# Projections of r, k and v in the scan as 64x64 quarters in two PSUM banks, added by VectorE; scratch ring of two banks instead of three

## Chip, cores and metric
One core of one Trainium2 chip. The metric is device time in microseconds (us); the kernel before takes 3047.45 us (median of 3 runs, 3044.28 to 3048.7).

## What is computed
A two-block network on 512 tokens of width 1024 (plus 256 context tokens), all in float32. Only the first block's scan is touched:

```python
# centred_shift: z[t-1]*w[0] + z[t]*w[1] + z[t+1]*w[2], over z = h @ w_in
r, k_f, k_b, v, d_f, d_b, kk, a_f, a_b, dg = rwkv_prep(centred_shift(z_rwkv, p["shift_conv"]), p)
# per token, 16 heads of 64, forward and backward:
S_new = S * d_t - (S @ kk_t) (kk_t * a_t)^T + v_t k_t^T
y     = S @ r_t           # forward: of S_new; backward: of S
```

The projection `h @ w_in` for r, k and v is a contraction over 1024 channels. The context needs k and v only. After the scan each head's y is centred, normalised, gets the bonus `sum(r*k*r_k) * v`, and is gated.

## The kernel before
`stage_scan` goes over 8 pairs of heads (`KT = 8`; a pair fills the 128 partitions, one head in each half). `TURNS` are 9 passes. Turn j solves pair j and meanwhile prepares pair b = j+1 and finishes pair a = j-1. A turn has 15 levels (s, l), s in 0..2 and l in 0..4. In each level TensorE, whose program is strictly in order, issues: a product (`multiply`, L759, into INV), the right side of a recurrence step beside scores (L861, L728), then `beside(j, (s, l, 0))`, then `solve` (L901, waits for ScalarE's `negate`, L1195), `correct` (L839, L841, waits for VectorE's `mask`, L1516), `read_out` (L928), then `beside(j, (s, l, 1))`; the next product waits for VectorE's `update` (L1527, L1529). At l = 4 there is no recurrence step; `correct_last` (L821) stands beside `x0` (L824). VectorE's own order is mask, its `beside(.,.,0)`, update, `state`, its `beside(.,.,1)`.

The projections are `project(b, which, piece)`, spread over TensorE's `beside` slots: K_X (k of the 512 tokens) at (0,0,1), (0,1,0), (0,1,1), (0,2,1), two channel groups each; K_V (k and v of the 256 context tokens) at (0,4,1), (1,0,1), (1,1,0), (1,1,1), four each; R_X (r), one group each at (1,4,0), (1,4,1), (2,0,1), (2,1,0), (2,1,1), (2,2,0) after two at (1,3,0); V_X (v) 3, 2 and 3 at (2,3,1), (2,4,0), (2,4,1). Each is a 128x128 matmul accumulating in bank PROJ (L680, L676). `bonus` (L951) follows the K_X piece at (0,1,0), `center` (L957) stands before the K_V piece at (0,4,1). VectorE's `shift` (L405, L408, L411; for K_V L1572, L1575, L1578) reads PROJ three times per projection: K_X at (0,3,0), K_V at (1,2,1), R_X at (2,2,1), V_X at (2,4,1). The next projection waits until all of it is done.

Everything else of TensorE goes through `Scratch` (L479), a ring of three banks: `take` waits until the use that had the bank before was read out ("moved"). A turn's uses in order: tokV0, score, par, score, bonus, score, rate 0 and 1, score, decay 0 and 1, tokB0, rate 2, decay 3, tokK0, x0, rate 3, decay 2, center, tokV1, score, var, tokB1, score, rstd, tokK1, score, gate, tokV2, score, ks, tokB2, x0, tokK2, inverse 0 and 1, scores(b) twice, x0. ScalarE reads tok (L1237), rate (L1213), decay (L1230), x0 (L1259) and center (L1316), VectorE the rest (score: L1600).

The rate and decay products (L643) are 64x64 matmuls with 512 or 256 columns, `w[H[d], half]` by `low[H[d], tokens]`; `H` are the two halves of the partitions, `O` the same two swapped.

Of the kernel before, what the change touches and what calls it, by code (L numbers as in the profile page):

```python
# [7 lines left out]
ALU = mybir.AluOpType  # L8
# [3 lines left out]
P = 128  # L12
T, TC, D = 512, 256, 1024
TA = T + TC
KT = D // P
# [494 lines left out]
def stage_scan(k, hT, w_low, low_loaded, th, da, sg, ya, spare, m, first_chunk, first_loaded, loose):  # L510
# [8 lines left out]
    bank = k.bank  # L519
# [4 lines left out]
    S = {n: k.sem("scan_" + n) for n in names}  # L524
    own_d, own_p = k.sem("scan_dve"), k.sem("scan_pool")
    H = [slice(HEAD * h, HEAD * h + HEAD) for h in range(2)]
    O = H[::-1]
# [3 lines left out]
    with ExitStack() as s:  # L531
        wj = first_chunk[:].rearrange("p j n -> p (j n)")[:, 0:3 * KT * P].rearrange("p (j i c) -> p j i c", j=KT, i=3)
# [18 lines left out]
        rkr = loose[:, 0:2 * T].rearrange("p (a t) -> p a t", a=2)  # L551
        hr = k.sb("head_r_k", [P, P], s)
# [7 lines left out]
        Z = k.sb("Z", [P, 2, 2, HEAD], s)  # L560
        yj, ysq = (loose[:, c:c + T] for c in (2 * T, 3 * T))
        rstd = k.sb("rstd", [P, 2 * NX], s)
        flat = spare[:].rearrange("p n c -> p (n c)")
        by_steps = lambda view: view.rearrange("p (n t) -> p n t", t=HEAD)
        per_step = lambda view: view.rearrange("p (n d c) -> p n d c", d=2, c=HEAD)
# [3 lines left out]
        U = flat[:, 5 * TA:5 * TA + P].rearrange("p (d c) -> p d c", d=2)  # L569
        rn = flat[:, 5 * TA + P:5 * TA + 2 * P].rearrange("p (d c) -> p d c", d=2)  # L570
        ZG = k.sb("ZG", [P, 2, HEAD], s)[:]
        Y, RU, INV, INVT, PROJ = (bank[i] for i in range(5))
        DZ = RU[:, 2 * P:3 * P]
        RIGHT = INVT[:, 2 * P:3 * P]
        sc = Scratch(k, "scratch", bank[5:8])
        block = s.enter_context(nc.Block())

        w_rkv = A["w_in"][0, :, 0:3 * D].rearrange("(i p) (s n c) -> p i s n c", p=P, s=3, n=KT)
# [17 lines left out]
        K_X, K_V, R_X, V_X = range(4)  # L596
        proj_no = lambda j, i: 4 * j + i + 1
        proj_bank = lambda j, i: Y if j == 0 and i in (K_V, V_X) else PROJ
        LOW_DECAY, LOW_RATE, LOW_GATE = range(3)
        low_bank = {LOW_DECAY: (INVT[:], INV[:, TC:2 * TC]), LOW_RATE: (RU[:], INV[:, 0:TC]), LOW_GATE: (RU[:], None)}  # L600
        low_no = lambda f: (6, 12, 15)[f]
        SHIFTED = 15
        shift_no = lambda j, i: SHIFTED * j + (3, 9, 12, 15)[i]

        def steps_of(j, s):

# [16 lines left out]
        def _(pe):  # L623
            mm = pe.matmul
# [32 lines left out]
            def project(j, which, piece, pieces=4):  # L657

                if not live(j):
                    return  # L660
                if piece == 0:
                    if which == K_X:
                        pe.wait_ge(S["wk_loaded"], 16 * (j + 1))
                    elif which == R_X:
                        pe.wait_ge(S["wr_loaded"], 16 * (j + 1))
                    elif which == K_V:
                        pe.wait_ge(S["wv_loaded"], 16 * (j + 1))
                    if j == 0 and which >= R_X:
                        pe.wait_ge(S["shift"], shift_no(0, which - 2))
                    elif j:  # L670
                        pe.wait_ge(S["shift"], shift_no(j, which - 1) if which else shift_no(j - 1, V_X))
                to = proj_bank(j, which)
                if which == K_V:
                    i, o = (1, to[:, 0:TC]) if piece < 2 else (2, to[:, TC:2 * TC])
                    for c in range(4 * (piece % 2), 4 * (piece % 2) + 4):
                        last = mm(o, wj[:, c, i, :], hT[:, c, T:TA], start=(c == 0), stop=(c == KT - 1))  # L676
                else:
                    i = {K_X: 1, R_X: 0, V_X: 2}[which]
                    for c in range(KT // pieces * piece, KT // pieces * (piece + 1)):
                        last = mm(to[:], wj[:, c, i, :], hT[:, c, 0:T], start=(c == 0), stop=(c == KT - 1))  # L680
                if piece == pieces - 1:
                    last.then_inc(S["proj"], 1)
# [264 lines left out]
            def bonus(j):  # L947
                if live(j):
                    pe.wait_ge(S["rk_done"], j + 1)
                    o = sc.take(pe, "bonus", j)  # L950
                    sc.fill(mm(o[:], hr[:], rkr[:, j % 2, :], start=True, stop=True), "bonus", j)  # L951

            def center(j):
                if live(j):
                    pe.wait_ge(S["y_copied"], j + 1)
                    o = sc.take(pe, "center", j)
                    sc.fill(mm(o[:], m["center"][:], yj[:], start=True, stop=True), "center", j)  # L957

            def variance(j):
                if not live(j):  # L960
# [26 lines left out]
            def beside(j, at):  # L987
# [4 lines left out]
                if at == (0, 0, 1):  # L992
                    project(b, K_X, 0)
# [514 lines left out]
        def _(dve):  # L1508
            tt, stt, ts = dve.tensor_tensor, dve.scalar_tensor_tensor, dve.tensor_scalar
# [45 lines left out]
            def shift(j, which):  # L1555

                if not live(j):
                    return
                dve.wait_ge(S["proj"], proj_no(j, which))
                mine = Steps(dve, S["shift"], shift_no(j, which - 1) if which else SHIFTED * j)  # L1560
                taps_of = lambda i: [col(j, 3 * t + i) for t in range(3)]
                z_of = proj_bank(j, which)
                if which == K_X:
                    if j:
                        dve.wait_ge(S["ke_done"], 2 * j)
                    shifted(mine, dve, [(kj[:, XS], z_of[:], T)], taps_of(1))
                elif which == K_V:
                    if j:
                        sc.settled(dve, "tokV", j - 1, 0)
                    parts_ = ((kj[:, CS], z_of[:, 0:TC], taps_of(1)), (vj[:, CS], z_of[:, TC:2 * TC], taps_of(2)))  # L1570
                    for dst, z, w in parts_:
                        mine.then(ts(dst, z, w[1], None, ALU.mult))  # L1572
                    mine.settle()
                    for dst, z, w in parts_:
                        mine.then(stt(dst[:, 1:TC], z[:, 0:TC - 1], w[0], dst[:, 1:TC], ALU.mult, ALU.add))  # L1575
                    mine.settle()
                    for dst, z, w in parts_:
                        mine.then(stt(dst[:, 0:TC - 1], z[:, 1:TC], w[2], dst[:, 0:TC - 1], ALU.mult, ALU.add))  # L1578
                    mine.settle()
                elif which == R_X:  # L1580
                    shifted(mine, dve, [(rj[:], z_of[:], T)], taps_of(0))
                else:
                    if j:
                        sc.settled(dve, "tokV", j - 1, 1)
                        sc.settled(dve, "tokV", j - 1, 2)
                    shifted(mine, dve, [(vj[:, XS], z_of[:], T)], taps_of(2))
# [102 lines left out]
            def gated(j):  # L1689
                if live(j):  # L1690
                    z = sc.read(dve, "gate", j)
                    dve.wait_ge(S["yn_done"], j + 1)
                    sc.free(stt(ya[:, j, :], yj[:], col(j, 13), z[:], ALU.add, ALU.mult), "gate", j)

            def beside(j, at):
                a, b = j - 1, j + 1
# [12 lines left out]
                if at == (1, 1, 1):  # L1709
                    normed(a)  # L1710
                if at == (1, 2, 1):
                    shift(b, K_V)
                if at == (1, 3, 0):
                    gated(a)
                if at == (1, 3, 1):
                    clamp(b)
                if at == (1, 4, 0):
# [1901 lines left out]
```

## Time and profile before

| | |
|---|---|
| median of 3 runs | 3047.45 us |
| profiled execution: its time / its span | 3037.74 us / 3036.0 us |
| TensorE, VectorE, ScalarE, GpSimd busy | 90%, 39%, 20%, 8% of the span |
| turns 0 to 6 of the scan | 135 to 833 us, about 100 us each |
| TensorE, VectorE busy in those | 92.59 and 60.30 us of each turn on average |

A row of the timeline says: start, length, engine, line, operation, out<-in, shape (rows x columns of the weights, then 64x512: partitions x moving columns), count merged in one row, and in brackets how long the engine was idle before it and what ended that. A float32 matmul stands as two MATMUL records (x2 is one matmul), each with its own weight load (PEld). A record's length includes the way through the array, so two that follow closely overlap.

### The profile page before, as it was taken

What the parts mean: (1) busy time and instruction counts of PE and PEld (TensorE: products, weight loads), DVE (VectorE), ACT (ScalarE), POOL (GpSimd) and SP (SyncE); (2) the same over time, 40 slices, a digit from 0 to 9 for tenths busy, and PEclk for the clock granted to TensorE, in tenths of its full rate; (3) what the DMA queues carried; (4) which work ended last, traced back from release to release, by engine and by line L of the source; (5) the groups of instructions that cost most, each with busy time, mean ns of one, the idle gap of its engine ahead of it and who ended that gap; (6) DMA issues with size and microseconds to landing.
All of it is one profiled execution on the core that took longest, in us unless ns stands there. A gap on an engine that the chain in (4) does not pass through costs nothing. (4 is left out here: it accounts for less than half of the span.)

```text
span 3036.0 us, 69543 instructions
## 1 busy us (share of the span) xinstructions
PE 2743.5 (90%) x31106; PEld 1489.7 (49%) x31106; DVE 1180.1 (39%) x2612; ACT 612.1 (20%) x1257; POOL 253.2 (8%) x283
## 2 busy tenths in 40 slices
PE   5899999999979999988988988988986998999998
PEld 3466666776664444444433433433333454455553
DVE  3565566566644762163221221211004245423333
ACT  3233323323321100010000000000002344322222
POOL 1220122112200000001000000000000111110000
PEclk9899999999999999998999999999997999999999
DMA  5000000000006871266999999999994311042210
GB/s 201 24 19 20 19 25 20 21 19 25 20 17 226 301 269 63 72 266 292 430 431 431 431 430 430 429 431 431 430 431 157 126 51 36 0 124 61 62 41 28
DMA packets 191501, 557.42 MB, mean 184 GB/s; under 512 B 32140, under 2 KB 119714, under 8 KB 166646
## 3 DMA queue, kind: packets, MB, share of 16 engines
q1 hardware_dynamic: 191222, 553.19, 46.6%
q8 instruction: 237, 3.88, 0.5%
q14 instruction: 42, 0.34, 0.0%
HBM read 550.65 MB, written 2.24 MB: 182 GB/s over the span
## 5 line engine op out<-in xcount | busy, mean ns | idle before, releaser
L2273 PE MATMUL bank<-arena,xe 128*64 128x512 f32 x1024 | 348.6, 607 | 37.4 <-DMA gates<-in_exp_w_dram 22.6
L680 PE MATMUL bank<-arena 128*128 128x512 f32 x384 | 199.6, 641 | 6.7 <-DVE vj L1578 5.3
L2273 PEld LDWEIGHTS bank<-arena,xe 128*64 128x64 f32 x1024 | 109.3, 140 | 186.8 <-issue 178.2
L3297 PE MATMUL bank<-arena 128*128 128x512 f32 x384 | 176.2, 607 | 3.4 <-PEq L78 3.4
L2273 PE MATMUL bank<-arena,hidT 128*64 128x512 f32 x512 | 170.0, 595 | 0.7 <-DMA gates<-in_exp_w_dram 0.5
L2726 PE MATMUL bank<-arena 128*128 128x512 f32 x320 | 146.4, 607 | 8.1 <-ACT arena L2887 8.1
L2273 PE MATMUL bank<-mg_ring,xe 128*64 128x512 f32 x256 | 116.2, 608 | 19.5 <-DMA u<-in_exp_w_dram 19.5
L2498 DVE TENSOR_TENSOR x<-x,bank 128x512 f32<-128x512 f32 x64 | 43.6, 686 | 230.1 <-PE bank L2311 230.1
L2273 PE MATMUL bank<-ys,xe 128*64 128x512 f32 x256 | 115.9, 607 | 17.8 <-DMA arena<-in_exp_w_dram 17.1
L2491 DVE TENSOR_TENSOR hid<-hid,bank 128x512 f32<-128x512 f32 x32 | 19.8, 682 | 284.4 <-PE bank L2273 284.4
L1516 DVE TENSOR_TENSOR pm<-bank,m_level 128x512 f32<-128x512 f32 x120 | 82.8, 690 | 118.1 <-PE bank L759 117.2
L839 PE MATMUL bank<-pm,XT 64*64 64x32 f32 x3072 | 107.9, 220 | 12.1 <-DVE pm L1516 9.5
L2273 PE MATMUL bank<-gates,xe 128*64 128x512 f32 x256 | 118.1, 616 | 0.0
L2273 PE MATMUL bank<-u,xe 128*64 128x512 f32 x256 | 116.6, 610 | 0.0
L841 PE MATMUL bank<-XT,pm 64*64 64x32 f32 x3072 | 111.5, 222 | 3.1 <-issue 3.1
L3297 PEld LDWEIGHTS bank<-arena 128*128 128x128 f32 x384 | 70.9, 192 | 84.2 <-issue 84.2
L759 PEld LDWEIGHTS bank<-X,px 64*64 64x64 f32 x2560 | 85.8, 135 | 48.9 <-issue 21.4
L759 PE MATMUL bank<-X,px 64*64 64x64 f32 x2560 | 98.3, 224 | 11.5 <-DVE XT L1529 6.5
L839 PEld LDWEIGHTS bank<-pm,XT 64*64 64x64 f32 x3072 | 100.3, 137 | 16.8 <-DVE pm L1516 11.6
L2726 PEld LDWEIGHTS bank<-arena 128*128 128x128 f32 x320 | 60.4, 195 | 82.4 <-issue 73.6
L841 PEld LDWEIGHTS bank<-XT,pm 64*64 64x64 f32 x3072 | 100.1, 136 | 1.5 <-issue 1.5
L680 PEld LDWEIGHTS bank<-arena 128*128 128x128 f32 x384 | 67.5, 196 | 63.1 <-issue 57.2
(523 smaller groups left out, 5513.8 us busy)
## 6 DMA issues: line engine op xcount, KB each, us to landing
arena<-in_exp_w_dram SPq DMA_DIRECT2D x96, 2048.0 KB, 26.7
gates<-in_exp_w_dram SPq DMA_DIRECT2D x24, 2048.0 KB, 29.5
ys<-in_exp_w_dram SPq DMA_DIRECT2D x24, 2048.0 KB, 26.0
mg_ring<-in_exp_w_dram SPq DMA_DIRECT2D x24, 2048.0 KB, 26.2
u<-in_exp_w_dram SPq DMA_DIRECT2D x24, 2048.0 KB, 30.7
ws_w<-in_ada_w_dram SPq DMA_DIRECT2D x40, 1024.0 KB, 5.3
arena<-in_odd_w_in_dram SPq DMA_DIRECT2D x32, 512.0 KB, 4.0
arena<-in_w_in_dram SPq DMA_DIRECT2D x24, 512.0 KB, 4.4
```

The costliest lines, as they stand in the source:

```text
L680: last = mm(to[:], wj[:, c, i, :], hT[:, c, 0:T], start=(c == 0), stop=(c == KT - 1))
L759: last = mm(INV[c, cs(q)], part(4 * g + q // 2, q % 2, 0, 0)[h], X[h, (j * GROUPS + g) % 2, q, :], start=True, stop=True)
L839: mm(into(INV, h, q), XT[c, g, q, :], blocks(pm[c, q, :], b, 0), start=True, stop=True)
L841: last = mm(into(INVT, c, q), pm[c, q, :], blocks(XT[c, g, q, :], b, 1), start=True, stop=True)
L1516: tt(pm[:], INV[:].rearrange("p (q t) -> p q t", q=8), m["level"][:, l, :].unsqueeze(1).to_broadcast([P, 8, HEAD]), ALU.mult).then_inc(S[" ...
L2273: r[e] = mm(out[a, :], lhs[j][:, a], w[:, j, 512 * c:512 * c + 512], start=(first and j == 0), stop=(last and j == len(lhs) - 1), skip_gro ...
L2491: dve.tensor_tensor(hid[:, f, :], hid[:, f, :], bank[4 + f][:], ALU.mult).then_inc(S["hid_made"], 1)
L2498: dve.tensor_tensor(x1[:, n, c], x1[:, n, c], bank[scatter_bank(q, o)][:], ALU.add).then_inc(S["added"], 1)
L2726: last = mm(o[:], w[:, c, i, :], hT[:, i, :], start=(i == 0), stop=(i == KT - 1))
L3297: last = mm(o[:], w[:, i, t, :], hT[:, t, :], start=(t == 0), stop=(t == KT - 1))
```

## The change
From the second pair on, each 128x128 projection matmul becomes four 64x64 ones: the two that stay in their half go to PROJ, the two that cross go to a second bank, PROJ2. `shift` first copies PROJ2 to SBUF (`zsum`), adds PROJ to it, and then does its three steps from `zsum`. The next projection waits only until the copy and the addition are done (`banks_read_no`). PROJ2 is bank 5, so `Scratch` has banks 6 and 7. `bonus` and `center` become two 64x64 matmuls each (their matrices are block diagonal). `gated` goes from VectorE's (1,3,0) to (1,2,1), ahead of the K_V shift. The first pair's projections in the prologue stay as they are.

```diff
+        zsum = k.sb("z_sum", [P, T], s)
-        Y, RU, INV, INVT, PROJ = (bank[i] for i in range(5))
+        Y, RU, INV, INVT, PROJ, PROJ2 = (bank[i] for i in range(6))
-        sc = Scratch(k, "scratch", bank[5:8])
+        sc = Scratch(k, "scratch", bank[6:8])
-        SHIFTED = 15
-        shift_no = lambda j, i: SHIFTED * j + (3, 9, 12, 15)[i]
+        FIRST_SHIFTS, SHIFTS = (3, 9, 12, 15), (5, 13, 18, 23)
+        shift_no = lambda j, i: FIRST_SHIFTS[i] if j == 0 else FIRST_SHIFTS[-1] + SHIFTS[-1] * (j - 1) + SHIFTS[i]
+        before_shift = lambda j, i: shift_no(j, i - 1) if i else shift_no(j - 1, V_X) if j else 0
+        banks_read_no = lambda j, i: before_shift(j, i) + 2 if j else shift_no(j, i)
...
-                        pe.wait_ge(S["shift"], shift_no(j, which - 1) if which else shift_no(j - 1, V_X))
+                        pe.wait_ge(S["shift"], banks_read_no(j, which - 1) if which else banks_read_no(j - 1, V_X))
+                if j:
+                    if which == K_V:
+                        i, out, tokens = (1, slice(0, TC), slice(T, TA)) if piece < 2 else (2, slice(TC, 2 * TC), slice(T, TA))
+                        channels = range(4 * (piece % 2), 4 * (piece % 2) + 4)
+                    else:
+                        i, out, tokens = {K_X: 1, R_X: 0, V_X: 2}[which], slice(0, T), slice(0, T)
+                        channels = range(KT // pieces * piece, KT // pieces * (piece + 1))
+                    for c in channels:
+                        for to, halves in ((PROJ, H), (PROJ2, O)):
+                            for rows, half in zip(H, halves):
+                                last = mm(to[half, out], wj[rows, c, i, half], hT[rows, c, tokens],
+                                          start=(c == 0), stop=(c == KT - 1), skip_group_check=True)
+                    if piece == pieces - 1:
+                        last.then_inc(S["proj"], 1)
+                    return
...
-                    sc.fill(mm(o[:], hr[:], rkr[:, j % 2, :], start=True, stop=True), "bonus", j)
+                    for h in H:
+                        last = mm(o[h, :], hr[h, h], rkr[h, j % 2, :], start=True, stop=True)
+                    sc.fill(last, "bonus", j)
...
-                    sc.fill(mm(o[:], m["center"][:], yj[:], start=True, stop=True), "center", j)
+                    for h in H:
+                        last = mm(o[h, :], m["center"][h, h], yj[h, :], start=True, stop=True)
+                    sc.fill(last, "center", j)
...
-                mine = Steps(dve, S["shift"], shift_no(j, which - 1) if which else SHIFTED * j)
+                mine = Steps(dve, S["shift"], before_shift(j, which))
-                z_of = proj_bank(j, which)
+                z_of = zsum if j else proj_bank(j, which)
+                if j:
+                    mine.last(dve.tensor_copy(zsum[:], PROJ2[:]))
+                    mine.last(tt(zsum[:], PROJ[:], zsum[:], ALU.add))
...
                 if at == (1, 2, 1):
+                    gated(a)
                     shift(b, K_V)
-                if at == (1, 3, 0):
-                    gated(a)
```

## Rows read from the trace of the kernel before

**Rows 1.** Windows, turn 3: length, then busy us (instructions) of each engine, TensorE clock.
```profile
437.70:537.80 100.10, 92.73 (x2789) 68.00 (x2783) 61.21 (x125) 33.79 (x68) 18.77 (x15) 0.98 0.08 22
```

**Rows 2.** Timeline, a slot with one 128x128 matmul of 512 columns between 64x64 ones.
```profile
407.12 0.40 PE L861 MATMUL bank<-Z,qr 64*64 64x64 f32 x8
407.45 1.12 PE L680 MATMUL bank<-arena 128*128 128x512 f32 x2
...
408.51 0.28 PE L901 MATMUL bank<-x,XT 64*64 64x64 f32 x2
```

**Rows 3.** Timeline, a slot with four 64x64 matmuls of 512 columns (rates), same neighbours.
```profile
350.65 0.28 PE L728 MATMUL bank<-qr,kt 64*64 64x128 f32 x2
350.76 1.02 PE L643 MATMUL bank<-da,a2j 64*64 64x512 f32 x6
351.47 0.34 PE L901 MATMUL bank<-x,XT 64*64 64x64 f32 x6
```

**Rows 4.** Timeline, a product (crossing halves) beside values (same halves), 64 columns each.
```profile
406.77 0.23 PE L759 MATMUL bank<-X,px 64*64 64x64 f32 x2
406.79 0.23 PE L944 MATMUL bank<-px,x 64*64 64x64 f32 x2
...
406.83 0.23 PE L759 MATMUL bank<-X,px 64*64 64x64 f32 x2
```

**Rows 5.** Timeline, level (0,1): end of the update and start of the next product.
```profile
446.96 0.42 DVE L1529 TENSOR_TENSOR XT<-XT,bank 128x256 f32<-128x256 f32 x1
...
448.60 0.27 PE L759 MATMUL bank<-X,pc 64*64 64x64 f32 x2
```

**Rows 6.** Groups by line and form, VectorE: count, then busy us, mean ns of one, idle before.
```profile
L186 DVE TENSOR_SCALAR arena<-ws_w,silu_c 128x512 f32<-128x512 f32 x20 | 9.7, 483 | 60.3 <-DMA ws_w<-in_ada_w_dram 60.3
L188 DVE SCALAR_TENSOR_TENSOR arena<-ws_w,silu_c,arena 128x512 f32<-128x512 f32 x120 | 90.2, 752 | 15.6 <-DMA ws_w<-in_ada_w_dram 11.0
L3470 DVE COPY na_k<-bank 128x512 f32<-128x512 f32 x8 | 5.5, 692 | 28.0 <-PE bank L3297 28.0
```

**Rows 7.** Timeline, level (0,3): first of the K_X shift's three steps, and the next product.
```profile
457.19 0.74 DVE L405 TENSOR_SCALAR kj<-bank,pcol 128x512 f32<-128x512 f32 x1
...
460.34 0.27 PE L759 MATMUL bank<-X,pc 64*64 64x64 f32 x2 [0.83 <-DVE XT L1529]
```

**Rows 8.** Timeline, K_V shift at (1,2,1) and what starts after it in (1,3).
```profile
487.13 0.48 DVE L1572 TENSOR_SCALAR kj<-bank,pcol 128x256 f32<-128x256 f32 x1
...
489.85 0.93 ACT L1264 ACTIVATE x<-kj,pcol 128x768 f32<-128x768 f32 x1 [4.77 <-DVE vj L1578]
...
489.97 1.95 PE L680 MATMUL bank<-arena 128*128 128x512 f32 x4 [0.83 <-DVE vj L1578]
...
491.85 0.39 PE L901 MATMUL bank<-x,XT 64*64 64x64 f32 x6
```

**Rows 9.** Waits of TensorE, 135 to 830 us: total us, times, longest us.
```profile
PE bank L839 <- DVE pm L1516: 9.3, 10, 1.7
```

**Rows 10.** Timeline, level (0,2): VectorE reads a score bank; first solve after the rate products.
```profile
450.68 0.69 DVE L1600 TENSOR_TENSOR px<-bank,m_part 128x512 f32<-128x512 f32 x1 [0.20 <-PE bank L728]
...
451.17 0.34 PE L901 MATMUL bank<-x,XT 64*64 64x64 f32 x6
```

**Rows 11.** Timeline, level (0,4): tokK0 on TensorE, reads on ScalarE, center.
```profile
461.70 1.10 PE L744 MATMUL bank<-m_id,kt 64*64 64x64 f32 x32
...
461.95 0.47 ACT L1213 ACTIVATE ra<-bank,pcol 128x256 f32<-128x256 f32 x1 [1.15 <-PE bank L643]
...
463.33 0.59 ACT L1311 ACTIVATE arena<-bank 128x512 f32<-128x512 f32 x1
...
464.56 1.10 PE L957 MATMUL bank<-arena,m_center 128*128 128x512 f32 x2 [0.32 <-ACT X L1259]
```

**Rows 12.** Timeline, level (2,0): the inverse's transposes, and ScalarE's copy of tokK2.
```profile
503.66 0.87 PE L702 MATMUL bank<-ident,x 128*128 128x128 f32 x6
503.95 0.59 ACT L1237 ACTIVATE tokK<-bank 128x512 f32<-128x512 f32 x1
```

## The prediction, made before the result was known
> **What bounds the kernel now.** The page first: the time is the span of one core. The windows of the scan next: a turn takes about 100 us, TensorE shows a record in 93 of them and VectorE in 61 [rows 1]. That looks like a kernel bound by TensorE, but a float32 record is long because of its way through the array, so a wait of up to 0.2 us between two records stays invisible, and the busy share does not say whose lateness decides. That is read level by level from the timeline: what started last before `correct` and before the next product. Two kinds of level appear. In most, TensorE comes late itself: at (0,1) VectorE's update ends at 447.38, the product starts at 448.60, after the K_X piece [rows 5]. There a shorter slot pays in full up to 1.2 us. In the levels that hold a `shift`, VectorE is late: at (0,3) the product waits for the update, which stood behind the shift [rows 7], and `correct` waits for the mask up to 1.7 us, 9.3 us over 10 times [rows 9]; these are the levels after the R_X and V_X shifts, whose three steps run ahead of the next mask. So the scan is a loop between TensorE and VectorE (with ScalarE's evictions in it), and an edit has to be priced in its level.
>
> **What the change takes away.** The 128x128 matmul between 64x64 ones. The last small record before it starts at 407.30 (407.12 + 0.40 less a record of 0.22), the next small one at 408.51: 1.21 us for one matmul [rows 2]. The four quarters of the rates do the same number of multiplications for 512 columns: the small record before them starts at 350.65, the next at 351.47, 0.82 us; the other pair of tiles is free 0.15 us later, so 0.82 to 0.97 us [rows 3]. A slot saves 0.24 to 0.39 us; I take 0.35, nearer to the first, because what follows is free to start on the pair that is free. The saving is per slot, not per matmul: it is the emptying of the array at both edges of the slot, and inside a slot both forms stream alike.
>
> A turn has 18 such slots with projections (K_X 4, K_V 4, R_X 7, V_X 3; `bonus` and `center` share two of them). Not gained: (1,1,0), where the transposes of `rstd` stay 128x128 and keep both edges; (1,3,0), which stands behind the K_V shift (priced below); (1,4,0), after which `x0` waits for GpSimd's work on XT anyway; (2,1,1) and (2,2,0), after which `correct` waits for VectorE's mask. That leaves 13 slots, 4.55 us. `bonus` uses only the tiles that stay in their half and the solve behind it only the crossing ones, so it overlaps: 0.3 us more. Gain 4.85 us a turn.
>
> **What it adds on VectorE.** Before each of four shifts a copy out of PSUM, 0.69 us, and an addition with one operand in PSUM (a mask of that kind takes as long), 0.69 us, with two settling waits of 0.035. Of the three steps the first gets cheaper with its source in SBUF, 0.48 instead of 0.74; the other two stay at 0.75 [rows 6, 7]. That is 1.45 - 0.26 = 1.19 us; upper bound 1.45 if the first step gains nothing. VectorE is busy for only 60% and could hide this, but not where it stands:
> - K_X at (0,3,0): between mask and update, the product already waits for it [rows 7]: 1.19 in full.
> - R_X at (2,2,1): ahead of mask (2,3), the longest wait of `correct` [rows 9]: 1.19.
> - V_X at (2,4,1): ahead of mask (0,0), `correct` just waits for it already: 1.19. (The shift itself starts earlier by what the three V_X slots save; that is in the gain.)
> - K_V at (1,2,1): before, 2.7 us from 487.13 to 489.85 [rows 8]. Now `gated` comes first (0.75), then copy and addition (1.42), then six steps of 256 columns at half the prices of rows 6, about 2.15: end at 491.45 instead of 489.82. Behind it are ScalarE's square of k (0.93) and, in ScalarE's order behind that, `negate` (0.28); the solve starts at 492.75 instead of 491.85 [rows 8]: 0.9. The earlier release of the banks (after the addition, at 489.3) lets R_X start 0.65 us earlier and buys nothing, since the solve waits for `negate`.
>
> Together 4.47 us a turn.
>
> **What two scratch banks add.** With three, a `take` waits for the use three before; with two, for the use two before. TensorE stops at that wait with all its program behind it. Going through the turn's list of uses:
> - (0,2): the rates take both banks at once, the second held by the score written just before. VectorE reads it from 450.68 to 451.37. The rates then start at 451.43 and need 0.9: the solve comes at 452.3 instead of 451.17 [rows 10]: 1.15 us, nothing hides it.
> - (0,4): tokK0 waits for the read of rate 2, to 462.42 (start 462.47 instead of 461.70); `x0` with `correct_last` follows 0.88 later, to 464.3. ScalarE then copies tokK0, Y and x0, 0.59 each, done at 465.4; only then rate 3 and decay 2 may be written, and `center` waits for the read of rate 3 (0.47) until 466.5. Before it started at 464.56 [rows 11]: 1.95 us.
> - (2,0): inverse 1 waits for ScalarE's copy of tokK2, to 504.54, and the array must empty behind it; solve at about 504.95 instead of 504.5 [rows 12]: 0.45.
> - (1,0): `var` waits for the copy of tokV1, the same kind with more between: an estimate of 0.3.
> - par at (0,0) waits for tokV0 and decay 1 at (0,3) for the score, 0.7 and 1.0 us, but in these two levels VectorE's shift is later still: 0. All other takes find the bank free by over 1 us. The move of `gated` is needed for the score at (1,3) and costs what stands above.
>
> Together 3.85 us a turn.
>
> **The sum.** 4.47 + 3.85 - 4.85 = 3.47 us a turn, 7 turns prepare a pair: 24 us. The projections bring four times the instructions (80 MATMUL records become 320, in a turn of 2789 [rows 1]); about 1 us more of stalls in issuing, and 1 us for the ring in the prologue: +26 us. Against the profiled execution 3037.74 + 26 = 3064; the median of the runs lies 9.7 above that execution, so 3073.5.
>
> **One rule set against the trace.** Both pairs of quarters write their two row halves into one bank. In the scan the product does this too (both halves into INV), beside `values` (both into Y): two records of each, four together, every 0.06 us [rows 4], and 64 columns are an eighth of the 0.43 us pass of 512, 0.054. So at 64 columns nothing is serialised. The rates do not test it at 512: each of their banks gets one row half.
> The Trainium skill, "TensorEngine Tiling (Array Packing)", Restrictions and Gotchas, says that different row tiles cannot access the same PSUM bank simultaneously; by this the pair would run one after the other. The trace disagrees at 64 columns; no row shows it at 512. It is the last of the rivals.
>
> **Rivals.**
> - *The ring does not bind.* If the takes find their banks read (readers earlier than the list says, or the stalls fall where TensorE would wait anyway), what is left is 4.47 against 4.85, and against up to 17 x 0.39 + 0.5 = 7.1 if every slot pays: -0.4 to -2.6 us a turn, 3 to 18 us faster, 3037 in the middle. It decides from the point where the ring costs under 0.4 us a turn. For it: most takes are far from binding. Against: (0,2), where the order of the program alone forces 1.15 us.
> - *Balance*: half the ring's cost and slots at 0.39 in nearly all places give 4.47 + 1.9 - 6.3 = 0: 3047.
> - *The edges stay*, the change does not do what it says: quarters of 512 columns mixed with small ones do not close up. Gain near 0: 8.3 x 7 = 58, 3106. Against: rows 3.
> - *Serialised pairs*: each of the 32 column blocks of 512 a turn (16 of 256 count half) takes 0.86 us more: 27.5 x 7 = 193, 3240.
>
> **Chances and range.** Slower as summed 0.70; ring not binding 0.17; balance 0.08; edges stay 0.03; serialised 0.02. Forecast 3073. Its own range by the bounds: gain 13 x 0.24 to 17 x 0.39, VectorE 4.3 to 5.9, ring 3.0 to 4.6: most of it within +9 to +45, 3056 to 3092. The range for 8 in 10 takes in the balance: 3045 to 3092. A difference under 0.2% (6 us) cannot be told from none. Slower by over 0.2% 0.75, within 0.2% 0.08, faster 0.17.
>
> **What would show it.** After: in each turn with projections, copy and addition of 0.69 before every shift; the product at (0,3) and `correct` at (2,3) and (0,0) later behind the shift by 1.2; small matmuls following a quarter slot without the 1.21; the rates at (0,2) starting only when the score is read, `center` about 2 us later after tokK0. The turn should take 103 to 104 us, TensorE's busy share lower. Wrong if the turn is shorter than 100 us, if the rates at (0,2) start within 0.2 us of the scores' end, or if a slot of quarters takes more than 1 us a channel.

## The result and the profile after

The changed kernel takes 3091.4 us (median of 4 runs, 3087.5 to 3096.71), the kernel before, run beside it, 3045.86 us (median of 4 runs). The ratio is 1.0166, 95% interval 1.0147 to 1.0185: 50 us slower, or 45.5 by the medians. The profiled execution took 3089.26 us with a span of 3087.5. Forecast were 26 us more: the direction was right, the size little more than half.

Below, us against the kernel before are the ratio less 1, times 3040. The expectations use differences of medians (58 for e2, 26 for e4), which lie up to 3 us off. A 95% interval reaches 4 to 9 us to either side.

Windows of the kernel after: the same columns as in [rows 1], turn 3 and then the seven turns that prepare a pair.

```profile
449.56:558.23 108.67, 92.90 (x3027) 69.37 (x3023) 64.03 (x132) 33.70 (x68) 18.55 (x15) 0.95 0.07 20
...
sum 746.89, PE 642.67 PEld 487.00 DVE 443.25 ACT 230.78 POOL 126.16; mean PE 91.81 PEld 69.57 DVE 63.32 ACT 32.97 POOL 18.02
```

From product to product of level (0,0) the seven turns of before add up to 699.45 us, those of after to 746.89: 6.8 us more a turn, where 3.47 were forecast (one profiled execution each; the one of before is 9.7 us faster than the median that the forecast starts from, the one of after 2 us faster than its own). TensorE's busy time falls by only 0.8 us a turn: the turn is longer because TensorE waits.

Three rows answer to [rows 2]. One channel group is now a slot of four small matmuls. The last small record ahead of it starts at 528.04 (527.81 + 0.45 less a record of 0.22), the next small one at 528.96: 0.92 us, inside the 0.82 to 0.97 that the rates' slot had given.

```profile
527.81 0.45 PE L946 MATMUL bank<-x 64*64 64x64 f32 x8
528.08 1.08 PE L685 MATMUL bank<-arena 64*64 64x512 f32 x8
528.96 0.25 PE L962 MATMUL bank<-qr,Z 64*64 64x64 f32 x2
```

Level (0,2), which answers to [rows 10]: VectorE reads the score from 468.22, the rates start only when it is done, and the solve follows 0.93 us after their start.

```profile
468.22 0.69 DVE L1625 TENSOR_TENSOR px<-bank,m_part 128x512 f32<-128x512 f32 x1 [0.45 <-PE bank L746]
...
469.05 1.09 PE L646 MATMUL bank<-da,a2j 64*64 64x512 f32 x8 [0.89 <-DVE px L1625]
...
469.98 0.34 PE L919 MATMUL bank<-x,XT 64*64 64x64 f32 x6
```

The K_X shift at (0,3), which answers to [rows 7]: copy and addition as priced, the first step 0.49, and the product waits 0.93 behind VectorE.

```profile
475.57 0.68 DVE L1586 COPY z_sum<-bank 128x512 f32<-128x512 f32 x1
...
476.28 0.69 DVE L1587 TENSOR_TENSOR z_sum<-bank,z_sum 128x512 f32<-128x512 f32 x1
...
477.01 0.49 DVE L405 TENSOR_SCALAR kj<-z_sum,pcol 128x512 f32<-128x512 f32 x1
...
479.91 0.27 PE L777 MATMUL bank<-X,pc 64*64 64x64 f32 x2 [0.93 <-DVE XT L1551]
```

And level (2,3), where it goes another way. Timeline of the kernel after, behind the R_X shift:

```profile
541.67 0.69 DVE L1587 TENSOR_TENSOR z_sum<-bank,z_sum 128x512 f32<-128x512 f32 x1
541.85 0.45 PE L919 MATMUL bank<-x,XT 64*64 64x64 f32 x8 [0.37 <-ACT x L1217]
542.39 0.49 DVE L405 TENSOR_SCALAR rj<-z_sum,pcol 128x512 f32<-128x512 f32 x1
542.91 0.75 DVE L408 SCALAR_TENSOR_TENSOR rj<-z_sum,pcol,rj 128x511 f32<-128x511 f32 x1
543.17 1.61 POOL L1469 TENSOR_TENSOR XT<-XT,m_pair 128x512 f32<-128x512 f32 x1 [10.34 <-ACT XT L1275]
543.70 1.63 DVE L411 SCALAR_TENSOR_TENSOR rj<-z_sum,pcol,rj 128x511 f32<-128x511 f32 x1
...
545.37 0.69 DVE L1538 TENSOR_TENSOR pm<-bank,m_level 128x512 f32<-128x512 f32 x1
546.11 0.32 PE L857 MATMUL bank<-pm,XT 64*64 64x32 f32 x2 [3.81 <-DVE pm L1538]
```

Two things stand in it that no step of the prediction has. The third step takes 1.63 instead of 0.75 us, beside GpSimd's work on XT. And `correct`, after a wait of 3.81 us, issues a small matmul with records of 0.32 us, not 0.22. The windows behind that wait give the granted clock (the column after POOL's; 1.00 is 2.4 GHz): 0.50, then 0.70. The whole of the first is at the lower level, 1.2 GHz.

```profile
546.11:549.00 2.89, 2.89 (x76) 2.44 (x80) 0.89 (x4) 0.00 (x0) 2.66 (x2) 0.50 0.00 0
549.00:552.00 3.00, 3.00 (x24) 1.42 (x20) 1.75 (x5) 0.00 (x0) 1.11 (x2) 0.70 0.00 0
```

In the kernel before the same two stretches, 522.50 to 528.10, are at full clock:

```profile
522.50:525.10 2.60, 1.91 (x74) 1.60 (x75) 1.34 (x4) 0.00 (x0) 2.52 (x3) 1.00 0.02 6
525.10:528.10 3.00, 3.00 (x55) 1.52 (x54) 2.97 (x6) 0.00 (x0) 2.13 (x1) 1.00 0.00 0
```

The Trainium skill, "TensorE: Matmul & The Clock Gate", section "HAM oscillation — how this bites in real kernels", tells of such a loop: a wait that recurs in each round drops TensorE to the slow clock, and the next piece starts slow each time. The trace agrees: the mean clock of the 3 us behind the wait at (2,3) is 0.50 to 0.52 in six of the seven turns and 1.00 in one, and the piece here is `correct` and the V_X slot.

TensorE's waits, 125 to 880 us of the kernel after (total us, times, longest). The first row answers to [rows 9], 9.3 us there; the second and third are the ring's and are new.

```profile
PE bank L857 <- DVE pm L1538: 23.7, 18, 3.8
...
PE bank L646 <- DVE px L1625: 12.8, 14, 1.2
...
PE bank L646 <- ACT X L1281: 5.9, 7, 0.9
```

Level by level, worked out from the starts of the products in the timeline (medians of turns 1 to 6, us), before | after | difference | forecast:

| level | before | after | diff | forecast |
|---|---|---|---|---|
| (0,0) | 6.45 | 7.40 | +0.96 | +0.84 |
| (0,1) | 8.14 | 7.28 | -0.87 | -1.0 |
| (0,2) | 5.97 | 6.86 | +0.89 | +0.80 |
| (0,3) | 5.78 | 6.92 | +1.14 | +1.19 |
| (0,4) | 6.98 | 8.73 | +1.75 | +1.6 |
| (1,0) | 6.56 | 7.25 | +0.68 | -0.05 |
| (1,3) | 7.23 | 8.25 | +1.01 | +0.9 |
| (1,4) | 5.56 | 4.61 | -0.95 | -0.35 |
| (2,3) | 9.00 | 12.17 | +3.17 | +0.84 |
| (2,4) | 6.86 | 6.16 | -0.70 | -0.70 |

The forecast column is the sum's terms put into their levels. The five levels left out differ from before by 0.3 or less; forecast were -0.35 at (1,1) and at (2,1), 0.10 at (2,0) and nothing at the other two. One level carries 2.3 of the 3.3 us a turn that were missed. Summed over the seven turns, (2,3) is 19.0 us longer where 5.9 were forecast, and (1,0) is 7.0 longer where 0.4 less was forecast; the cleanest gain of the quarters is (0,1), 0.87 us shorter in six turns of seven for two slots and `bonus` (forecast 1.0).

### The profile page after: what moved, and what is told of

It reads as the page before. It is cut to its first block and busy times, and to the rows that moved or that the text cites. A ratio compares the mean times of both kernels' runs of the same rounds, so it can differ in the third digit from the quotient of the medians.

```text
span 3087.5 us, 73023 instructions
## 1 busy us (share of the span) xinstructions
PE 2745.2 (89%) x32818; PEld 1503.9 (49%) x32818; DVE 1204.3 (39%) x2668; ACT 612.3 (20%) x1257; POOL 251.3 (8%) x283
## 5 line engine op out<-in xcount | busy, mean ns | idle before, releaser
L2297 PE MATMUL bank<-arena,xe 128*64 128x512 f32 x1024 | 350.3, 608 | 30.9 <-DMA gates<-in_exp_w_dram 19.7
L685 PE MATMUL bank<-arena 64*64 64x512 f32 (+1 forms) x2240 | 251.9, 546 | 3.5 <-issue 2.4
L3321 PE MATMUL bank<-arena 128*128 128x512 f32 x384 | 175.5, 605 | 3.4 <-PEq L78 3.4
L2750 PE MATMUL bank<-arena 128*128 128x512 f32 x320 | 147.0, 609 | 8.1 <-ACT arena L2911 8.1
L857 PE MATMUL bank<-pm,XT 64*64 64x32 f32 x3072 | 114.2, 224 | 30.0 <-DVE pm L1538 25.1
L2297 PE MATMUL bank<-ys,xe 128*64 128x512 f32 x256 | 116.1, 607 | 16.1 <-DMA arena<-in_exp_w_dram 15.4
L685 PEld LDWEIGHTS bank<-arena 64*64 64x64 f32 x2240 | 103.5, 142 | 51.5 <-issue 44.2
L777 PE MATMUL bank<-X,px 64*64 64x64 f32 x2560 | 105.0, 228 | 11.0 <-DVE XT L1551 5.3
L777 PEld LDWEIGHTS bank<-X,px 64*64 64x64 f32 x2560 | 94.6, 140 | 37.5 <-DVE XT L1551 18.2
L3321 PEld LDWEIGHTS bank<-arena 128*128 128x128 f32 x384 | 70.5, 191 | 84.0 <-issue 84.0
L2750 PEld LDWEIGHTS bank<-arena 128*128 128x128 f32 x320 | 60.7, 195 | 82.8 <-issue 74.0
## 6 DMA issues: line engine op xcount, KB each, us to landing
gates<-in_exp_w_dram SPq DMA_DIRECT2D x24, 2048.0 KB, 29.8
```

Of the source, the lines that this page charges most:

```text
L685: last = mm(to[half, out], wj[rows, c, i, half], hT[rows, c, tokens], start=(c == 0), stop=(c == KT - 1), skip_group_check=True)
L777: last = mm(INV[c, cs(q)], part(4 * g + q // 2, q % 2, 0, 0)[h], X[h, (j * GROUPS + g) % 2, q, :], start=True, stop=True)
L857: mm(into(INV, h, q), XT[c, g, q, :], blocks(pm[c, q, :], b, 0), start=True, stop=True)
L2297: r[e] = mm(out[a, :], lhs[j][:, a], w[:, j, 512 * c:512 * c + 512], start=(first and j == 0), stop=(last and j == len(lhs) - 1), skip_gro ...
L2750: last = mm(o[:], w[:, c, i, :], hT[:, i, :], start=(i == 0), stop=(i == KT - 1))
L3321: last = mm(o[:], w[:, i, t, :], hT[:, t, :], start=(t == 0), stop=(t == KT - 1))
```

## The experiments

**First: do the three terms add up, and which is wrong?**

e1_ring2: two scratch banks and the moved `gated`, nothing else.

```diff
-        sc = Scratch(k, "scratch", bank[5:8])
+        sc = Scratch(k, "scratch", bank[6:8])
```

> The kernel before with a scratch ring of two banks (bank 5 left unused) and gated moved to (1,2,1); nothing else. Theory A (the terms of the prediction add up, each right): ring 3.85 us a turn, a little for gated ahead of the K_V shift (0.75 us, partly hidden), 7 turns: +27 to +32 us. Theory B (the terms are right alone, but only together they make TensorE wait so long that its clock falls, and that is the missing 20 us): the same +27 to +32 here, with half-clock stretches as before. Theory C (the ring itself was mis-priced, also in the turn without a next pair): +40 us or more.

Measured: 3065.6 us, ratio 1.0093 (1.0065 to 1.0121), +28 us. The ring's term (27) was right. The rates' wait for the score is there with its 0.9 us in both of its levels:

```profile
PE bank L643 <- DVE px L1600: 12.4, 14, 0.9
```

e2_vector: whole 128x128 projections, three banks, but copy and second operation on VectorE, steps from `z_sum`.

```diff
+                    mine.last(dve.tensor_copy(zsum[:], PROJ[:]))
+                    mine.last(tt(zsum[:], PROJ[:], zsum[:], ALU.max))
```

> The kernel before (128x128 projections, three scratch banks) with the copy and a second VectorE pass of the same kind (maximum of PROJ and its own copy, so the result stays) ahead of each shift, and the early release of the bank after them. Theory A: 3 x 1.19 and 0.5 to 0.9 at the K_V shift, 7 turns: +28 to +31 us. Theory B: the same or a little more: TensorE's wait before correct at (2,3) grows from 1.7 to 2.9 us; if the clock falls there already, +35 to +45. Theory C (VectorE's cost was right): +30 and nothing at (2,3) beyond 1.2 us.

Measured: 3098.0 us, ratio 1.0182 (1.0163 to 1.0201), +55 us, against 31 forecast. This is the wrong term.

e3_quarters: only the quarters that stay in their half, in one bank, without copy and addition; three banks, and `gated` back at (1,3,0).

```diff
-                        for to, halves in ((PROJ, H), (PROJ2, O)):
+                        for to, halves in ((PROJ, H),):
...
-                    mine.last(dve.tensor_copy(zsum[:], PROJ2[:]))
-                    mine.last(tt(zsum[:], PROJ[:], zsum[:], ALU.add))
```

> The two quarters of each projection that stay in their half, in PROJ, three scratch banks, no VectorE copy or addition, bonus and center as in the changed kernel. The two crossing quarters are left out, so half of the contraction is missing from r, k and v; the pass over the array is as long for two quarters as for four, if four run side by side. Theory A and B: 13 to 17 slots save 0.35 us a turn, 7 turns: -30 to -40 us. Rival (the edges stay): within 5 us of before.

Measured: 3005.72 us, ratio 0.9887 (0.9871 to 0.9904), -34 us: 4.9 us a turn, as the prediction had it in the sum (4.85). Not in the places: in the traces (2,3) alone gives 16.0 us in seven turns and (0,0) 13.0, where 2.5 each were forecast, and (1,2), (2,4) and (0,3) are 6.4, 6.9 and 4.4 longer. How much of this is low clock of the kernel before, gone here, was not isolated. Since this form has half the matmuls in flight, it is no proof that the crossing pair costs nothing; the slot of 0.92 us above is.

28 + 55 - 34 = 49, and the whole change measured 50. By this sum the 24 us of the error lie in VectorE's term. But the agreement is partly luck, since level by level the three do not add up. Over seven turns of the traces the three together give 20.5 us at (0,3), 26.5 at (0,4) and 3.2 at (2,3); the changed kernel has 8.0, 12.2 and 19.0. One reason is shown further down: e2 stretches the third step of the k shift, which the changed kernel does not. So where the changed kernel loses its time is read from its own levels, and e2 only says that VectorE's work costs more than its price.

e4_vx_early: the first V_X slot goes ahead of `correct` at (2,3), into TensorE's wait.

```diff
-                if at == (2, 3, 1):
+                if at == (2, 3, 0):
                     for i in range(3):
                         project(b, V_X, i, KT)
```

> The changed kernel with the first three V_X pieces at (2,3,0) instead of (2,3,1), in the wait for the mask behind the R_X shift. Theory A (only the waits count): 2.6 us of projections move under a wait of 3 to 4 us: 7 x 2.6 = 18 us faster than the changed kernel, about +27 against before. Theory B (the clock falls in that wait and stays at half for the levels behind it): the wait is filled, the clock stays, 7 x 4 to 5 = 28 to 35 us faster than the changed kernel, about +10 to +17 against before.

Measured: 3066.13 us, ratio 1.0090 (1.0073 to 1.0106), +27 us: 23 us of the 50 are gone with one slot moved. (2,3) takes 7.99 us instead of 12.17, (2,4) 7.79 instead of 6.16. The row that was 23.7 us with a longest wait of 3.8 is now:

```profile
PE bank L857 <- DVE pm L1538: 7.9, 14, 1.3
```

The time is what theory A had (+27, only the wait counts, V_X work of 2.6 us a turn moves under it), and theory B's number (+10 to +17) was missed. The clock did come back: behind (2,3) it is 1.00 in all seven turns. But (2,3) and (2,4) together are only 19.7 us shorter in seven turns, because at (2,4) `correct_last` now waits for VectorE's mask, 1.15 us in five turns of seven. So e4 says where the missing time is, but not which of three things it is: the wait itself, the stretched third step, or the clock.

**Second: the stretched step or the clock?**

Rows of the groups by line and form, 125 to 880 us, for the third step: first of e2, then of the kernel after (whose k step stays at 0.75 in every turn), then of e6_psum_source below.

```profile
L411 DVE SCALAR_TENSOR_TENSOR kj<-z_sum,pcol,kj 128x511 f32<-128x511 f32 x7 | 11.5, 1636 | 0.2
L411 DVE SCALAR_TENSOR_TENSOR rj<-z_sum,pcol,rj 128x511 f32<-128x511 f32 x7 | 9.7, 1391 | 0.2
```

```profile
L411 DVE SCALAR_TENSOR_TENSOR rj<-z_sum,pcol,rj 128x511 f32<-128x511 f32 x7 | 7.9, 1129 | 0.2
```

```profile
L411 DVE SCALAR_TENSOR_TENSOR kj<-bank,pcol,kj 128x511 f32<-128x511 f32 x7 | 5.2, 750 | 0.2
L411 DVE SCALAR_TENSOR_TENSOR rj<-bank,pcol,rj 128x511 f32<-128x511 f32 x7 | 5.2, 750 | 0.2
```

e6_psum_source: e2, with the steps reading PSUM as before, so that only copy and second operation are added.

```diff
-                z_of = zsum if j else proj_bank(j, which)
+                z_of = proj_bank(j, which)
```

> As e2_vector (the copy and the addition alone, three scratch banks, whole 128x128 projections), but the three shift steps read PROJ in PSUM as in the kernel before, and the next projection waits for all of them. Theory that the SBUF source makes VectorE and GpSimd collide: the last step takes 0.75 us in every turn (in e2 1.64 for k and 1.39 for r on average), 0.89 + 0.64 saved a turn, against 0.26 more in each first step (three on the path): -5 us over seven turns by these alone, and the wait at (2,3) is about 0.4 us shorter, so that the clock falls in fewer turns, up to 10 us more: 43 to 53 us above before, against 58 for e2. Rival (the stretched steps are not on the path, only the price of the source counts): 5 us more than e2, 63 above before. If the last step is still stretched beside GpSimd's work on XT, it is not the source.

Measured: 3096.02 us, ratio 1.0192 (1.0165 to 1.0220), +58 us. The step is back to 0.75 in every turn, so the source does it, and the time is not better than e2's. The theory was right on the step and wrong on what it is worth. The levels say why: (0,3) and (1,3) are longer by 1.45 us, the work added, but (0,0) by 3.13 and (2,3) by 3.65. TensorE waited 3.2 us at (2,3) where it had waited up to 1.7 before, and in the window behind that wait the clock is:

```profile
545.49:548.49 3.00, 2.75 (x73) 2.63 (x74) 0.94 (x4) 0.00 (x0) 2.84 (x2) 0.50 0.02 5
```

e9_work_only: e6, and the two waits filled with matmuls that nobody reads.

```diff
+                if at in ((2, 3, 0), (0, 0, 0)) and ...:
+                    pe.wait_ge(S["r_neg"], ...)
+                    for i in range(10 if at[0] else 6):
+                        for c in H:
+                            mm(INVT[c, 0:P], m["id64"][c], hT[c, 0, 0:P], ...)
```

> As e6_psum_source (copy and addition alone, every later step 0.75 us; 58 us above before), with idle 64x64 matmuls of 128 columns (results never read) in the two waits of TensorE before correct: 10 pairs at (2,3,0), 6 at (0,0,0). Clock theory: what is left is VectorE's own work, 1.45 us at each of four shifts in seven turns, 5.8 x 7 = 41 us above before, (2,3) at 9.7 to 9.9 us instead of 12.65 and (0,0) at 7.9 instead of 9.58. Rival (the clock is not what stretches the two levels): both stay as long, 58 us above before.

Measured: 3079.11 us, ratio 1.0150 (1.0129 to 1.0170), +46 us; 41 was expected by the clock, 58 by its rival. (2,3) takes 9.74 us and (0,0) 7.90: both are 1.45 above the shortest turns of before (8.29 and 6.45), the added work and nothing else. VectorE has the same instructions as in e6; what differs is the idle matmuls and TensorE's clock behind them. The window behind the same wait, and the sum of the waits for the mask, which was 29.8 us with a longest of 3.2 in e6:

```profile
533.50:536.50 3.00, 3.00 (x88) 2.15 (x79) 1.71 (x6) 0.28 (x1) 2.92 (x3) 1.00 0.02 5
```

```profile
PE bank L842 <- DVE pm L1524: 8.0, 12, 1.2
```

e5b_warm: the same cure in the changed kernel, at (2,3,0) alone.

```diff
+                if at == (2, 3, 0) and live(b) and b:
+                    pe.wait_ge(S["shift"], banks_read_no(b, R_X))
+                    for i in range(12):
+                        for rows, half in zip(H, O):
+                            mm(PROJ2[half, 0:P], m["id64"][rows], hT[rows, 0, 0:P], ...)
```

> The changed kernel, with 12 idle pairs of 64x64 matmuls of 128 columns (results in PROJ2, never read) put at (2,3,0), into TensorE's wait of 3.8 us before correct. Clock theory: the granted clock in the 3 us behind that wait is 1.0 again instead of 0.50 and 0.70; correct takes 1.14 us instead of 1.94 and the V_X slot 2.6 instead of 4.0. That is up to 2.2 us in a turn; over the turns in which the clock fell (41 us of the scan more at the low clock than before, so 20 us at most, part of it hidden) 10 to 14 us faster than the changed kernel: 32 to 38 us above the kernel before. Rival (the low clock costs nothing there, VectorE's lateness decides alone): no shorter than the changed kernel, 46 to 52 us above before, or longer by what the idle matmuls take.

Measured: 3072.16 us, ratio 1.0123 (1.0098 to 1.0147), +37 us: 13 us back, for 2.6 us of useless work on TensorE in each turn. (2,3) falls from 12.17 to 9.44, which is 1.15 above the 8.29 of the shortest turns of before; the prediction had 1.19 for R_X there, less 0.35 for the slot. In the first two turns the level still holds another stall of 1.2 us, as in the changed kernel, and yet it takes 9.4 and 9.5 us instead of 12.3 and 12.2. The third step still averages 1.03 us, so the stretch is not what went. `correct` and what follows, at 535.40:

```profile
535.40:538.40 3.00, 3.00 (x101) 2.18 (x101) 1.54 (x6) 0.28 (x1) 2.92 (x3) 1.00 0.02 5
```

**Third: can the change be saved, or the kernel before improved?**

e7_act_copy: e4, and ScalarE does the copy of PROJ2 to `z_sum`, at (0,3,0), (1,2,0), (2,2,1) and (2,4,1) of its own order.

```diff
-                    mine.last(dve.tensor_copy(zsum[:], PROJ2[:]))
+                    dve.wait_ge(S["zcopy"], 4 * (j - 1) + which + 1)
...
+                    f(zsum[:], PROJ2[:], ACT.Copy).then_inc(S["zcopy"], 1)
```

> As e4_vx_early (the changed kernel with the first V_X slot ahead of correct at (2,3); 26 us above before), with the copy of PROJ2 done by ScalarE instead of VectorE. If VectorE's lateness at the four shifts sets the time, each copy of 0.69 us leaves the path: 4 x 0.69 x 7 = 19 us less, 5 to 9 us above before. Rival (ScalarE's own work is late behind the copy, above all its square of k and negate at (1,2)): of that only the k, r and v shifts at (0,3), (2,3), (0,0) pay and (1,2) costs 0.6 more: 14 - 4 = 10 us less, 16 above before.

Measured: 3061.24 us, ratio 1.0081 (1.0060 to 1.0102), +25 us, where e4 had 27. Both theories missed: they had 9 and 16. Where VectorE was late, the levels are shorter than in e4: (0,3) by 0.64, (1,3) by 0.74, (2,3) by 0.84, (0,0) by 0.25 in the median, together 15.4 us in seven turns. It is given back at (0,4), (1,0), (2,1) and (2,4), together 15.7 us in seven turns, up to 3.7 us in a single one. VectorE now waits for ScalarE's copy (5.8 us in 125 to 880). Why the other four levels grow was not isolated.

e8_reordered: e7, with the last K_X piece ahead of the rates and the first K_V piece ahead of tokK0.

```diff
-                if at == (0, 2, 1):
+                if at == (0, 2, 0):
                     project(b, K_X, 3)
-                if at == (0, 2, 0):
+                if at == (0, 2, 1):
                     both_directions(b, "rate")
...
+                    project(b, K_V, 0)
                     to_tokens(j, "K", 0)
```

> As e7_act_copy, with two orders changed on TensorE: the last K_X piece at (0,2,0) and the rates at (0,2,1), so that the rates' take of both banks has the score read by then; and the first K_V piece ahead of tokK0 at (0,4), so that its take finds rate 2 read. Ring theory: (0,2) was 0.9 to 1.2 us longer with two banks and (0,4) 1.75 to 2.8; about 1.1 us of each is hidden by this: 16 us less than e7, 7 to 12 us faster than the kernel before. Rival (the rates come later on ScalarE, and decay and GpSimd behind them; the K_V piece delays x0): nothing gained or some us lost against e7, 5 to 15 above before.

Measured: 3047.73 us, ratio 1.0030 (1.0015 to 1.0046), +9 us. The 16 us against e7 came as expected ((0,2) 5.62 instead of 6.85, (0,4) 7.90 instead of 9.06); but e7 itself had stayed 17 us above its forecast, and so the kernel before is not reached. The rates' wait is met half as often:

```profile
PE bank L646 <- DVE px L1635: 6.2, 7, 0.9
```

e11_reordered_filled: e8 with 6 idle pairs at (0,0,0), as in e9.

> As e8_reordered (9 us above before), with 6 idle pairs at (0,0,0). In e8 only one turn of six has a long level there (7.66 against 7.19) and 9 of the 38 us at the low clock: clock theory 0 to 3 us less, 6 to 9 above before. Rival (e8's distance comes from the clock): before's time is reached or beaten. What stays would then be VectorE's addition and the ring, 0.7 to 0.9 us in each of (0,0), (0,3), (0,4) and (1,0), against the slots.

Measured: 3038.77 us, ratio 1.0013 (1.0001 to 1.0026), +4 us, between 0 and 8 by the interval: the 6 to 9 expected are not excluded, and the 5 us less than e8 are no more than the noise of the two. In the trace (0,0) became longer, 7.66 instead of 7.19, and what is shorter are levels that the idle pairs don't touch, so nothing here speaks for the pairs. With everything tried, the quarters in two banks came level with the kernel before and not ahead of it.

e10_before_filled: the kernel before with 6 idle pairs at (2,3,0) and (0,0,0).

> The kernel before with 6 such idle pairs at (2,3,0) and at (0,0,0), nothing else changed. Clock theory: its levels (2,3) and (0,0) lie at 8.29 and 6.45 us in their shortest turns and 9.4 us above these in all six turns together; with the waits filled they stay at the short ones: 6 to 11 us faster than before. Rival (the long turns come from something else, or before's waits of 1.7 us are harmless): same time within 2 us, or slower where the idle matmuls delay the solve (0.1 to 0.3 us a turn, 1 to 4 us).

Measured: 3032.06 us, ratio 0.9986 (0.9974 to 0.9998), -4 us. That is less than the 6 to 11 expected. (2,3) sits at 8.29 in the median instead of 9.00, but (0,0) rises from 6.45 to 7.17: there TensorE had no wait to fill, and the pairs delay the solve.

e12_before_one_fill: the same at (2,3,0) alone.

```diff
+                if at in ((2, 3, 0), ) and ...:
+                    pe.wait_ge(S["r_neg"], ...)
+                    for i in range(6):
+                        for c in H:
+                            mm(INVT[c, 0:P], m["id64"][c], hT[c, 0, 0:P], ...)
```

> The kernel before with 6 idle pairs at (2,3,0) alone. In e10_before_filled the pairs at (2,3,0) brought the level from 9.00 to 8.29 us in the median (3.7 us in six turns together), while those at (0,0,0) lengthened their level in the usual turn from 6.45 to 7.17 (4.3 us in six turns), more than the two long turns of before (4.7 us) had to give. By this the pairs at (2,3,0) alone give 4 to 8 us: 4 to 8 us faster than before, and no slower than e10. Rival: 6 us is as much as two executions differ by the irregular stalls, and nothing can be told from before.

Measured: 3029.88 us, ratio 0.9965 (0.9952 to 0.9979), -11 us. The interval is -15 to -6, and 4 to 8 faster were expected. It is faster than both kernels, by work that is thrown away: the kernel before already lost time here. Its windows follow, turns 3 and 4 (clock 1.00 in both) and the sum of seven (699.45 before). Turn 3 is 1.3 us shorter than in [rows 1], but not by the idle pairs: its (2,3) takes 9.12 us instead of 8.29, and its (1,4), ahead of them, 5.34 instead of 7.95. What fits the pairs is elsewhere: (2,3) gives 3.5 us in seven turns, and (0,0) in the two turns that follow the first two filled waits 4.7 (6.47 and 6.45 instead of 9.72 and 7.89). Another 4.0 us lie in (1,4) and 2.2 in the first (0,0), which comes ahead of all idle pairs; nothing here gives these to the pairs.

```profile
416.96:515.76 98.80, 93.36 (x2803) 68.78 (x2802) 62.13 (x124) 33.80 (x68) 18.83 (x15) 1.00 0.08 22
515.76:615.51 99.75, 93.59 (x2803) 68.91 (x2802) 61.88 (x124) 33.91 (x68) 18.81 (x15) 1.00 0.08 22
...
sum 687.09, PE 647.99 PEld 478.32 DVE 426.69 ACT 231.61 POOL 131.00; mean PE 92.57 PEld 68.33 DVE 60.96 ACT 33.09 POOL 18.71
```

## Why the prediction was right in direction and wrong in size

- **What the quarters save**: right in the sum, 4.85 us a turn forecast (34 us), 34 in e3, though e3 gains it in other levels than forecast, so the agreement is in part luck. The mechanism is seen in the changed kernel: the slot takes 0.92 us, (0,1) is 0.87 shorter; both pairs of quarters run side by side at 512 columns, so the edges do go away and nothing is serialised.
- **What two banks cost**: right in the sum, 3.85 us a turn forecast (27 us), 28 measured. Inside it, (0,4) was 2.76 in e1 instead of 1.95, (0,2) 1.24 instead of 1.15, and the waits at (1,0) and (2,0) cost nothing.
- **What VectorE adds**: this step failed, 4.47 us a turn (31 us) against 55 in e2. The prices of copy, addition and first step were right (0.68, 0.69, 0.49). K_V's six steps were not half of the others: 0.35 and 0.48 us each, 2.6 together instead of 2.15. While the clock stayed up the levels came near their prices: 1.14 at (0,3), 1.01 at (1,3), 1.15 at (2,3) in e5b. What failed is the line "R_X at (2,2,1): ahead of mask (2,3), the longest wait of `correct`: 1.19". I used that row to show that VectorE's lateness counts in full there, and stopped. The longest wait of the loop grew from 1.7 to as much as 3.8 us, and in six turns of seven TensorE came out of this level's waits at half clock. (2,3) became 19.0 us longer in seven turns instead of 5.9. In turn 3 of the changed kernel that made `correct` 1.94 us long and the V_X slot 4.0 instead of 2.6.
- **The size of that**: filling the wait gives back 13 us in the changed kernel (50 to 37) and 13 in the VectorE-only kernel (58.4 to 45.6). Each difference of two ratios is uncertain by 9 to 10 us. The traces (one execution each) put it at the same place: over seven turns (2,3) is 17.1 us shorter in e5b than in the changed kernel, and 18.3 in e9 than in e6, where (0,0) gives 10.0 more.
- **The rest of the 24 us**: open. The stretched third step, 0.88 us in three turns of seven, is 3 us at most. (1,0) is 7.0 us longer in the seven turns, by stalls of up to 2 us in which TensorE waits for nothing that the trace shows. They fall differently in each kernel: with the wait at (2,3) taken away they are nearly gone in e4 and e5b, but e7, where it is taken away too, is 6.9 us longer there than e4, and e2 and e6, which have the long wait, are not longer there than the kernel before. The last turn, which prepares nothing, is 5.2 us longer from its first product to its last (77.7 against 72.5), but that is no mark of the change: it lies between 72.5 and 80.2 in all the traces, and at 78.4 in e12, the fastest of the kernels that compute the whole result. These parts were read from the traces, not tested.
- **The rivals**: none held the real course. They priced instructions and waits; none asked what a longer wait does to the engine that waits. The kernel before had the clue in its own rows: its (2,3) takes 8.29 us in some turns and 9.98 in others with the same instructions, because behind a wait of 1.74 us the clock was down in three turns of four. I took the average. Two of the four, the second low and the last at full clock:

```profile
320.32:323.32 3.00, 2.99 (x73) 2.56 (x74) 1.14 (x4) 0.00 (x0) 2.92 (x3) 0.54 0.03 5
...
523.20:526.20 3.00, 3.00 (x76) 2.12 (x77) 1.77 (x5) 0.00 (x0) 2.92 (x3) 1.00 0.02 5
```

## What to carry to other kernels

A wait costs its length and, when it grows, it can cost the clock of the work behind it. Before pricing a change that makes the longest recurring wait of TensorE longer, look at the granted clock in the windows just behind that wait, in several rounds: if it is already down in some, expect the longer wait to put it down in nearly all (here from three turns of seven to six). Moving real work into the wait gave the most here (23 us in e4), idle matmuls less (13 us in e5b, 11 in e12), and they cost time where TensorE had no wait to fill ((0,0) in e10).

Splitting a matmul to fit its neighbours' tile shape paid here as calculated (34 us), but two halves that must be added put the cost onto another engine, at the places where that engine is already late.

## What the runs showed of the hardware that I had not expected

- The granted clock of TensorE fell and rose within one turn of the loop, behind its waits but not by the length of the longest alone. Behind waits of 3.1 to 3.8 us at (2,3) the mean clock of the next 3 us was 0.50 in twelve of thirteen turns (kernel after, e2, e6), and it was as low in three turns of the kernel after that had shorter waits (1.4 to 1.7 us) and another stall of 0.9 to 1.3 us in the same level, but 1.00 in a fourth with 1.14 and 1.43 us; behind 1.74 us it was 0.54 to 0.77 in three turns and 1.00 in one in the kernel before, 0.60, 0.63 and three times 1.00 in e1; with the wait filled 1.00 in all seven, in e5b, e9, e10 and e12.
- VectorE's `scalar_tensor_tensor` with both tensors in SBUF takes 0.75 us alone and up to 1.64 beside a GpSimd TENSOR_TENSOR, which itself takes 1.61 instead of 1.27. With one of the two in PSUM it takes 0.75 in every turn of e6 and of before. The Trainium skill, "SBUF — State Buffer", section "SBUF: two separate sides", says that a VectorE operation with two SBUF inputs and a GpSimd operation that reads SBUF lock each other out for the whole instruction. The trace agrees in direction (how long each was held up differs from turn to turn): moving the source of the shift from PSUM to SBUF saved 0.26 us in the first step and opened the last one to this.
- The two pairs of quarters write different partition halves of the same bank from different row halves, 512 columns each, without one waiting for the other (0.92 us for four).
